# A decoder block in one kernel: the MLP's up product by Strassen's seven block products, with the squared values stored to DRAM and read back for the down product

## The chip, the cores and the metric

The kernel is one program on one core of a Trainium2 chip. It uses TensorE (PE, matmuls into PSUM), VectorE (DVE), ScalarE (ACT), and SyncE (SP) as the queue that issues the DMAs. GpSimd (POOL) only prepares constants. The metric is device time in microseconds, the median of several executions. One more execution was profiled; the rows below come from it.

## What is computed

A hybrid decoder block over 1024 tokens of width 1024: two attention mixers side by side, gates, an output projection with a residual, and an MLP with squared ReLU and a residual. The change touches the second half:

```python
mixed = jax.nn.sigmoid(ga) * ya + jax.nn.sigmoid(gb) * yb
x = x + mixed @ w_out[l]                       # (1024, 1024) @ (1024, 1024)
h = _rms_norm(x, norm_mlp_g[l])                # y * rsqrt(mean(y * y) + 1e-6) * g
x = x + jnp.square(jax.nn.relu(h @ w_up[l])) @ w_down[l]   # 1024 -> 4096 -> 1024
return _rms_norm(x, norm_final_g)
```

All tensors are float32.

## The kernel before

**Data.** Everything is held transposed: 128 features on the partitions, 1024 tokens along the free dimension, so the width of 1024 is eight chunks of 128x1024. `kp` (in `keep`) is the residual in that form, chunk m at `kp[:, m, :]`. A matmul takes a 128x128 weight block and moves 512 tokens (one PSUM bank). PSUM is four tensors `PS[0]` to `PS[3]` of two banks each.

**Precision.** Each operand is split in a high part (a cast to fp32r on ScalarE, `split_hi2`, `mlp_in_hi`) and a low part (value minus high part, on VectorE, `split_lo2`). A product takes three matmuls: high by high, high by low, low by high. So a 1024-deep product of 128 output features for 1024 tokens is 8 x 3 x 2 = 48 matmuls.

**Output projection.** Eight chunks n. Per chunk TensorE transposes a column chunk of x (`x_chunk`, L775), then runs the 48 matmuls (`split_products`, L529). ScalarE copies the transposed x to `kp` (L1143). VectorE adds the product (L1477), ScalarE squares the chunk (L1153), VectorE adds the square to an accumulator (L1485). Chunks 0 to 3 of the MLP's input are split as they come, 4 to 7 after the last chunk (L1136, L1480), since their place is the projection's input until then. Weights come through a ring of four slots (`raw_at`, `wsp_at`).

**MLP.** Eight blocks of 512 hidden features. In a block, four hidden chunks j (L529; the very first by `products_by_chunk`, L518, which takes the input chunks one by one), alternately in `PS[0]` and `PS[1]`. VectorE takes the ReLU and scales by the inverse root mean square (L1496); ScalarE squares (L1164) and casts (L1167); VectorE makes the low part (L1499). Then the down products of these four hidden chunks: for each of eight output chunks m 24 matmuls into `PS[2 + m % 2]` (L837), which VectorE adds to `kp` (L1511). The blocks after the first stand in a loop. The mean square is two 512-column matmuls with a constant matrix (`mean_square`, L798), which leaves the mean on all partitions; then a root on ScalarE (L1156) and a 1024-wide reciprocal on VectorE (L1488).

**The end.** In the last block VectorE also sums the squares of the result (L1516, squares L1178). Eight one-column matmuls give the mean per token (L851), `kp` is transposed back (L857), VectorE scales (L1531), and SyncE stores.

**What sets the order.** It is written out by hand. Each engine runs its own list in order, and the lists meet at semaphores: `w_hi`, `w_lo` (weights split), `w_used` (a chunk's products done), `resid`, `acc_ok`, `u_r`, `u_hi`, `u_lo`, `dn_add`. An instruction that waits holds up all behind it on its engine, and the same holds for SyncE's list of DMAs.

## Time and profile before

| | us |
|---|---|
| median of three runs | 1749.26 (1747.21 to 1750.57) |
| the profiled execution, its own time | 1750.55 |
| its span, first to last instruction | 1748.4 |
| TensorE busy / VectorE busy / ScalarE busy | 1669.4 / 862.9 / 682.0 |
| output projection to the end of the last down product | 931.3 to 1725.9 |
| mean granted TensorE clock | 0.987 |

The span counts from the first to the last instruction, the execution's own time also what lies around it. The granted clock is the share of full speed (2.4 GHz) that TensorE was allowed; 0.50 is 1.2 GHz. Busy time of TensorE is that of pipelined matmuls with modelled ends, so the distance between starts in the chain of waits tells more of its pace than the mean duration of one.

### The profile page before, as it was taken

How to read it: one execution, taken by the hardware profiler on the slowest of the kernel's cores; microseconds unless marked ns; L12 is line 12 of the kernel's file. 1: busy time of each engine (PE TensorE's matmuls, PEld its weight loads, DVE VectorE, ACT ScalarE, POOL GpSimd, SP SyncE). 2: the span in 40 equal slices, each digit the busy share in tenths (PEclk: the TensorE clock that was granted, in tenths of full speed). 3: DMA queues.
4: the chain of work that ended last, by engine and by line, in shares of the span. 5: the costliest groups of instructions: out<-in, count | busy, mean ns of one | idle time of the engine just before them, and what ended most of it. 6: DMA issues, size and time to landing. Idle time of an engine off the chain costs nothing.

```text
span 1748.4 us, 22421 instructions
## 1 busy us (share of the span) xinstructions
PE 1669.4 (95%) x8188; PEld 1372.0 (78%) x8188; DVE 862.9 (49%) x1738; ACT 682.0 (39%) x1484; POOL 4.1 (0%) x20
## 2 busy tenths in 40 slices
PE   6999898897999999999999999999999999999997
PEld 5777677674788887788888888888888888888886
DVE  5788888865666666421226344232323333333345
ACT  6467767773666666411114222121212121212121
POOL 0000000000000000000000000000000000000000
PEclk9999999997899999999999999999999999999999
DMA  5210100110020100112123302111111111111102
GB/s 181 78 33 25 37 25 25 37 37 1 13 61 26 49 13 22 34 43 57 42 76 101 109 26 72 49 48 48 48 48 48 48 48 48 48 48 48 36 12 96
DMA packets 126109, 84.93 MB, mean 49 GB/s; under 512 B 2888, under 2 KB 122696, under 8 KB 125904
## 3 DMA queue, kind: packets, MB, share of 16 engines
q1 hardware_dynamic: 126032, 83.94, 16.0%
q8 instruction: 44, 0.72, 0.2%
q14 instruction: 33, 0.27, 0.0%
HBM read 79.70 MB, written 4.23 MB: 48 GB/s over the span
## 4 chain that ended last, share of the span: by engine, by line
PE 81%; DVE 9%; ACT 5%; issue 4%; DMA 0%; ACTq 0%; DVEq 0%; SPq 0%
PE ps L529 36%; PE ps L837 20%; PE ps L573 12%; PE ps L645 4%; PE ps L612 2%; DVE work L1281 2%; PE ps L623 2%; PE ps L518 1%; ACT work L994 1%; DVE ps L1302 1%; DVE o_nat L1324 1%; ACT tmp L986 1%; DVE tmp L1266 1%; DVE work L1309 1%; ACT tmp L950 1%
## 5 line engine op out<-in xcount | busy, mean ns | idle before, releaser
L573 PE MATMUL ps<-hspl,wsp 128*128 128x512 f32 x1536 | 426.3, 411 | 8.3 <-ACT tmp L950 6.6
L573 PEld LDWEIGHTS ps<-hspl,wsp 128*128 128x128 f32 x1536 | 268.1, 191 | 55.0 <-ACT tmp L950 8.4
L529 PE MATMUL ps<-hspl,wsp 128*128 128x512 f32 x1176 | 276.3, 392 | 0.6 <-ACT keep L1016 0.6
L529 PEld LDWEIGHTS ps<-hspl,wsp 128*128 128x128 f32 x1176 | 222.4, 189 | 47.1 <-issue 0.8
L837 PE MATMUL ps<-hspl,wsp 128*128 128x512 f32 x768 | 177.4, 390 | 0.0
L837 PE MATMUL ps<-hspl,work 128*128 128x512 f32 x768 | 175.4, 389 | 0.0
L1511 DVE TENSOR_TENSOR keep<-keep,ps 128x1024 f32<-128x1024 f32 x64 | 78.2, 1221 | 193.5 <-PE ps L837 192.5
L837 PEld LDWEIGHTS ps<-hspl,wsp 128*128 128x128 f32 x768 | 143.6, 188 | 32.6 <-DVE keep L1511 2.6
L837 PEld LDWEIGHTS ps<-hspl,work 128*128 128x128 f32 x768 | 144.2, 188 | 29.9
L529 PE MATMUL ps<-work,wsp 128*128 128x512 f32 x648 | 153.5, 390 | 0.0
L645 PEld LDWEIGHTS ps<-work 128*128 128x128 f32 x856 | 112.5, 192 | 47.9 <-issue 38.2
L645 PE MATMUL ps<-work 128*128 128x128 f32 x856 | 122.9, 277 | 21.3 <-DVE o_nat L1324 20.3
L529 PEld LDWEIGHTS ps<-work,wsp 128*128 128x128 f32 x648 | 121.7, 188 | 25.7 <-issue 0.5
L1164 ACT ACTIVATE tmp<-tmp 128x1024 f32<-128x1024 f32 x32 | 33.9, 1060 | 264.4 <-DVE tmp L1496 264.4
L529 PE MATMUL ps<-hspl,work 128*128 128x512 f32 x576 | 136.9, 390 | 0.0
L986 ACT ACTIVATE tmp<-ps,negmax 128x128 f32<-128x128 f32 (+7 forms) x160 | 87.5, 547 | 125.8 <-DVE negmax L1302 124.1
L1309 DVE TENSOR_TENSOR work<-ps,work 128x128 fp32r<-128x128 f32 (+3 forms) x192 | 84.5, 454 | 102.6 <-ACT work L994 100.0
L529 PEld LDWEIGHTS ps<-hspl,work 128*128 128x128 f32 x576 | 107.8, 188 | 22.2
L1496 DVE SCALAR_TENSOR_TENSOR tmp<-ps,tmp 128x1024 f32<-128x1024 f32 x32 | 39.2, 1224 | 172.5 <-PE ps L529 172.5
L969 ACT ACTIVATE work<-tmp 64x128 fp32r<-64x128 f32 x320 | 113.2, 354 | 5.9
L1281 DVE SCALAR_TENSOR_TENSOR work<-tmp,work 64x128 fp32r<-64x128 f32 x320 | 101.3, 316 | 9.3 <-ACT work L969 1.8
L529 PE MATMUL ps<-work 128*128 128x512 f32 x384 | 92.2, 389 | 0.0
(158 smaller groups left out, 1737.7 us busy)
## 6 DMA issues: line engine op xcount, KB each, us to landing
raw<-in_w_in SPq DMA_DIRECT2D x47, 512.0 KB, 3.6
raw<-in_w_up SPq DMA_DIRECT2D x16, 512.0 KB, 4.0
tmp<-in_w_up SPq DMA_DIRECT2D x16, 512.0 KB, 4.0
raw<-in_w_down SPq DMA_DIRECT2D x16, 512.0 KB, 3.3
tmp<-in_w_down SPq DMA_DIRECT2D x16, 512.0 KB, 3.3
keep<-in_x SPq DMA_DIRECT2D x8, 512.0 KB, 6.6
fbias<-f_rows SPq DMA_DIRECT2D x8, 512.0 KB, 5.0
tmp<-in_x SPq DMA_DIRECT2D x8, 512.0 KB, 4.4
```

The lines of the kernel that those rows point to most:

```text
L529: ins = pe.matmul(ps[:, cols], w(wp, k), mv(mp, k)[:, cols], start=(k == 0 and n == 0), stop=(k == ks - 1 and n == 2))
L573: ins = pe.matmul(psp(u, g), wsp[:, c % 2, wp, k * P:(k + 1) * P], hspl[:, mp, k, cols], start=(n == 0), stop=(n == 23), skip_group_check= ...
L612: ins = pe.matmul(oo, lt, rh, start=(m == 0), stop=(m == len(ops) - 1), skip_group_check=True)
L623: ins = pe.transpose(PS[2][:, (u % 2) * HALF + (k - a) * P:(u % 2) * HALF + (k - a + 1) * P], probs(G)[:, k * P:(k + 1) * P], ident[:])
L645: ins = pe.matmul(o, pt[:, G % 2, part, n * P:(n + 1) * P], v_nat[:, j, s % 2, :, :].rearrange("p s d -> p (s d)"), start=(part == 0 and n ...
L837: ins = pe.matmul(PS[2 + m % 2][:, cols], wsp_at(m // 2, wp)[:, a:a + P], hid[:, mp, f, cols], start=(f == 0 and n == 0), stop=(f == 3 and ...
L969: act.activation(tile_view(q_st[dst:dst + 64, G % 3, 0, :], t), tile_tokens(q_raw(t)[row:row + 64], t, s // 2), ACT.Copy, scale=-QSCALE).t ...
L986: act.activation(probs(G)[:, 0:n * P], psc[G % 2][:, 0:n * P], ACT.Exp, bias=negmax[:, c:c + 1], scale=-1.0, accum_out=rowsum[:, c:c + 1]) ...
L1281: dve.scalar_tensor_tensor(out=tile_view(q_st[dst:dst + 64, G % 3, 1, :], t), in0=tile_tokens(q_raw(t)[row:row + 64], t, s // 2), scalar=- ...
L1309: dve.tensor_tensor(pt[:, G % 2, 1, a * P:b * P], PS[2][:, (u % 2) * HALF:(u % 2) * HALF + (b - a) * P], pt[:, G % 2, 0, a * P:b * P].bitc ...
L1496: dve.scalar_tensor_tensor(out=tmp[:, 0, :], in0=PS[j % 2][:], scalar=0.0, in1=tmp[:, 3, :], op0=ALU.max, op1=ALU.mult).then_inc(u_r, 1)
L1511: dve.tensor_tensor(kp[:, m, :], kp[:, m, :], PS[2 + m % 2][:], ALU.add).then_inc(dn_add, 1)
```

## The change

**Up product.** The 1024x1024 input H is taken as 2x2 blocks: feature chunks k and k + 4 (k = 0 to 3), left and right 512 tokens. The weights of two neighbouring hidden chunks (q, 16 such pairs) are 2x2 blocks too: a11, a12 for the first chunk and a21, a22 for the second, each 512 x 128. Instead of eight block products (96 matmuls) there are seven of 12 matmuls each, P1 to P7, in Winograd's form with 4 sums of weights (s1 to s4, `sums`), 4 sums of H (`h_t1` to `h_t4`, once), and 7 sums of results. Some sums of results are made by TensorE itself, which adds a product to what the bank holds; the others by `copy_s1`, `copy_s2`, `copy_s3` on ScalarE and `up_c22`, `up_c12` on VectorE. The product order of each q reaches over three pairs (`up_products`). All sums of the weights and of H are made of whole values, then split in a high and a low part (`form_hi`, `form_lo`, `h_hi`, `h_lo`).

**Hidden values.** After the ReLU with the scale (`up_r..`, VectorE) and the square (`square_..`, ScalarE) each 128x512 quarter is stored to the DRAM tensor `hidden`. `kp` serves as room for these, so the residual chunks are stored to `x_mid` in the output stage and read back (`reload`) after the up stage.

**Down stage.** After all of the up stage, eight blocks of four hidden chunks, read from DRAM and split again (`hidden_hi`, `hidden_lo`). The 24 matmuls per output chunk and block stay; they go through all four PSUM tensors in turn, and an add has three further chunks' time.

**Inverse root.** The mean square is eight one-column matmuls with the squares as weights; the root and the reciprocal work on 128x8; eight fp32 matmuls of the broadcast column with the identity (`spread_rstd`) put it on all partitions.

**Output stage.** The chunk order is 0, 4, 1, 5, 2, 6, 3, 7, so pairs k, k + 4 become ready and their sums are made on the way. The weights use two slots. The last chunk runs with k outermost and frees `hspl` piece by piece (`o_used`) for the forms t13 and t4b. The MLP loops are written out instead of looped. The stages before the output projection keep their instructions and order.

Core of the diff:

```diff
+def up_products(n):
+
+    if n == 0:
+        order = [(0, P1), (0, P2), (0, P6), (0, P5)]
+    elif n < UP:
+        order = [(n, P1), (n - 1, P7), (n - 2, P3), (n, P6), (n - 1, P4), (n, P2), (n, P5)]
+    else:
+        order = [(n - 1, P7), (n - 2, P3), (n - 1, P4), (n - 1, P3)]
+    return [x for x in order if x[0] >= 0]
...
+            for n in range(UP):
+                q = n + 2
+                if q < UP:
...
+                if n >= 1:
+                    store_u22(n - 1)
+                if q < UP:
...
+                        sp.wait_ge(a_lo, A_FORM[n, 2])
+                    load_a(q, "a21")
+                    if n == 1:
+                        sp.wait_ge(hf_lo, H_FORM["t4b", 3])
+                    load_a(q, "a22")
+                elif n == UP - 1:
+                    sp.wait_ge(done, PRODUCT[UP - 1, P6])
+                    load_hidden(2)
+                    load_hidden(3)
+                if n >= 2:
+                    store_u12(n - 2)
+                if n >= 1:
+                    store_u21(n - 1)
+                sp.wait_ge(done, PRODUCT[n, P2])
+                if q < UP:
+                    load_a(q, "a12")
...
                 if n == 0:
-                    products_by_chunk(PS[0], ring_w(0), h_at, m_lo, 0).then_inc(w_used, 1)
+                    products_by_chunk(PS[0], w_of(c), h_at, m_lo, 0).then_inc(w_used, 1)
                     x_chunk(0)
-                else:
-                    split_products(PS[n % 2], ring_w(n), h_at, KC).then_inc(w_used, 1)
+                elif n < KC - 1:
+                    split_products(PS[n % 2], w_of(c), h_at, KC).then_inc(w_used, 1)
+                else:
+                    for k in range(KC):
+                        for half in range(2):
+                            cols = slice(half * HALF, (half + 1) * HALF)
+                            for i, (wp, mp) in enumerate(((0, 0), (0, 1), (1, 0))):
+                                ins = pe.matmul(PS[n % 2][:, cols], w_of(c)(wp, k), h_at(mp, k)[:, cols],
+                                                start=(k == 0 and i == 0), stop=(k == KC - 1 and i == 2),
+                                                skip_group_check=True)
+                        if k == KC - 1:
...
                 pe.wait_ge(xres, KC)
+                for i in range(8):
+                    ins = pe.matmul(PS[2][:, i:i + 1], tmp[:, 1, i * P:(i + 1) * P], mean_w[:, 0:1], start=True, stop=True)
+                ins.then_inc(mean_done, 1)
...
+            def spread_rstd():
+
+                pe.wait_ge(rstd_ok, 1)
+                for i in range(8):
+                    ins = pe.matmul(PS[2][:, i * P:(i + 1) * P], xrstd[:, i:i + 1].broadcast_to((P, P)), ident[:],
+                                    start=True, stop=True)
...
+            def product(q, j):
+
+                b = form_place(j)[0]
+                pe.wait_ge(a_lo, A_FORM[q, b])
+                if j == P1:
+                    if q < 2:
+                        pe.wait_ge(resid, KC - 1)
+                    else:
+                        pe.wait_ge(c21_ok, q - 1)
+                elif j == P2 and q < 2:
+                    pe.wait_ge(xres, KC)
+                elif j in (P2, P6):
+                    pe.wait_ge(s1_ok, q + 1)
+                elif j == P5:
+                    if q < 2:
+                        pe.wait_ge(resid, KC)
+                    elif q < 4:
+                        pe.wait_ge(rstd_out, 1)
+                    else:
+                        pe.wait_ge(c12_ok, q - 3)
+                elif j == P7:
+                    pe.wait_ge(s2_ok, q + 1)
+                elif j == P4:
+                    pe.wait_ge(s3_ok, q + 1)
+                else:
+                    pe.wait_ge(c22_ok, q + 1)
...
+                    if q == 0:
+                        pe.wait_ge(hf_lo, H_FORM[{P1: "b11", P2: "b21", P6: "t2", P5: "t13", P7: "t13", P4: "t4b",
+                                                  P3: "t4b"}[j], k])
+                    for m, (wp, mp) in enumerate(((0, 0), (0, 1), (1, 0))):
+                        ins = pe.matmul(o, a_part(q, j, wp)[:, k * P:(k + 1) * P], b_block(j, mp, k),
+                                        start=((j in (P1, P5) or j == P2 and q < 2) and k == 0 and m == 0), stop=(k == 3 and m == 2),
+                                        skip_group_check=True)
+                ins.then_inc(done, 1)
+
+            for n in range(UP + 1):
+                for q, j in up_products(n):
+                    product(q, j)
+                    if (q, j) == (0, P6):
+                        mean_square()
+                    if (q, j) == (1, P1):
...
+
+            for i in range(8 * FF_BLOCKS):
+                b, g = i // 8, i // 2
+                o = PS[DN_BANKS[i % 4]]
...
+                elif i == 3:
+                    pe.wait_ge(c12_ok, UP)
+                else:
+                    pe.wait_ge(dn_add, i - 3)
...
-            with pe.Fori(1, FF_BLOCKS) as b:
-                mlp_block(b, False)
-
+                    for f in range(4):
+                        if i % 8 == 0 and half == 0:
+                            pe.wait_ge(dh_lo, 4 * b + f + 1)
+                        for n, (wp, mp) in enumerate(((0, 0), (0, 1), (1, 0))):
+                            a = f * 256 + (i % 2) * P
+                            ins = pe.matmul(o[:, cols], dn_w[g % 4][:, wp, a:a + P], dn_h[(4 * b + f) % 8][:, mp, cols],
+                                            start=(f == 0 and n == 0), stop=(f == 3 and n == 2))
+                ins.then_inc(dn_done, 1)
 
             pe.wait_ge(facc, KC)
...
+            for n in range(KC):
+                m = OUT_ORDER[n]
+                act.wait_ge(xct_done, n + 1)
+                act.wait_ge(m_lo, KC if n else 1)
+                act.copy(kp[:, m, :], PS[2 + n % 2][:]).then_inc(xres, 1)
+                if n >= 1:
+                    scale(n - 1)
+                if n in (2, 4, 6):
+                    for what in ("b11", "b21", "t2"):
+                        h_hi(what, n // 2 - 1)
+                if n + 2 < KC:
+                    split_hi(CH_OUT + n + 2)
+                if n == 3:
+                    for b in range(3):
+                        form_hi(0, b)
...
+            for k in range(3):
+                h_hi("t13", k)
+            h_hi("t4b", 0)
+            form_hi(1, 0)
+            scale(KC - 1)
+            h_hi("b21", 3)
+            copy_s1(0)
+            h_hi("t2", 3)
+            square_mid(KC - 1)
+            h_hi("t13", 3)
+            copy_s2(0)
+            act.wait_ge(mean_eps, 1)
+            act.activation(xstat[:], xstat[:], ACT.Sqrt).then_inc(mean_root, 1)
+            form_hi(1, 1)
+            for k in range(1, 4):
+                h_hi("t4b", k)
+            act.wait_ge(rstd_done, 1)
+            act.copy(kp[:, 0, :], PS[2][:]).then_inc(rstd_out, 1)
...
+            for n in range(1, UP):
+                copy_s1(n)
+                if n + 1 < UP:
+                    form_hi(n + 1, 0)
+                else:
+                    weights_hi(0)
+                    weights_hi(1)
+                copy_s3(n - 1)
+                square_22(n - 1)
...
+            def sums(q):
+
+                a = {x: a_block(q, x) for x in ("a11", "a12", "a21", "a22", "s1", "s2", "s3", "s4")}
+                dve.wait_ge(a_in[q % 4], 64 * (q // 4 + 1))
+                if q >= 2:
...
+            def residual(n):
+                m = OUT_ORDER[n]
                 dve.wait_ge(w_used, CH_OUT + n + 1)
                 dve.wait_ge(xres, n + 1)
-                dve.tensor_tensor(kp[:, n, :], kp[:, n, :], PS[n % 2][:], ALU.add).then_inc(resid, 1)
...
+            for n in range(KC - 1):
+                if n in (2, 4, 6):
+                    k = n // 2 - 1
+                    h_t2a(k)
+                    h_t2b(k)
+                    h_lo("b11", k)
+                    h_lo("b21", k)
+                    h_t4(k)
+                    h_lo("t2", k)
+                    h_t1(k)
...
+                        form_lo(0, b)
+                residual(n)
+                if n + 2 < KC:
+                    split_lo(CH_OUT + n + 2)
+                add_square(n)
+            h_lo("b11", 3)
+            for k in range(3):
+                h_lo("t13", k)
+            h_lo("t4b", 0)
+            sums(1)
+            form_lo(1, 0)
+            residual(KC - 1)
+            h_t2a(3)
+            h_lo("b21", 3)
+            h_t2b(3)
+            h_t4(3)
+            h_lo("t2", 3)
+            h_t1(3)
+            h_t3(3)
+            add_square(KC - 1)
+            h_lo("t13", 3)
...
+            def up_c12(q):
+                dve.wait_ge(done, PRODUCT[q, P3])
+                dve.wait_ge(s2_ok, q + 1)
+                after(dve, u12_out, 16 * q)
+                add(u12, bank_c(q), s2[q % 2]).then_inc(c12_ok, 1)
...
+            for n in range(1, UP):
+                if n + 1 < UP:
+                    sums(n + 1)
+                up_c22(n - 1)
+                if n + 1 < UP:
+                    form_lo(n + 1, 0)
+                else:
+                    weights_lo(0)
+                    weights_lo(1)
+                up_r22(n - 1)
+                if n >= 2:
+                    up_c12(n - 2)
+                form_lo(n, 2)
+                if n >= 2:
+                    up_r12(n - 2)
+                up_r21(n - 1)
+                if n + 1 < UP:
+                    form_lo(n + 1, 1)
+                else:
+                    hidden_lo(0)
+                    hidden_lo(1)
+                up_r11(n)
+            hidden_lo(2)
...
+            weights_lo(3)
+            for g in range(4 * FF_BLOCKS):
+                pair = DN_PAIRS[g % 4]
+                if g + 4 < 4 * FF_BLOCKS:
+                    hidden_lo(g + 4)
+                if 2 <= g and g + 2 < 4 * FF_BLOCKS:
```

The places where the order of instructions changed most follow. Names: `up_b`, `up_t` are split sums of H; `a_hi`, `a_lo` the split weight forms; `hf_lo`, `a_lo`, `s1_ok`, `done` semaphores.

TensorE before, from the end of the output projection, through the mean square, into the second up chunk:

```order
L529 MATMUL ps<-hspl,work 128x512 x47
L518 MATMUL ps<-work,wsp 128x512 [waits h_lo,w_lo,resid]
L518 MATMUL ps<-work,wsp 128x512 x5
...
L518 MATMUL ps<-hspl,wsp 128x512 [waits h_lo]
L518 MATMUL ps<-hspl,wsp 128x512 x5
L798 MATMUL ps<-tmp,mean_w 128x512 [waits xres,acc_ok]
L798 MATMUL ps<-tmp,mean_w 128x512
L529 MATMUL ps<-work,wsp 128x512 [waits w_lo,resid]
```

TensorE after, the product P2 of q = 0 (its last piece of H), the start of P6, then the start of P1 of q = 1 and the spread:

```order
L1084 MATMUL ps<-up_b_60,a_hi_0_71 128x512 [waits hf_lo]
L1084 MATMUL ps<-up_b_60,a_hi_0_71 128x512
L1084 MATMUL ps<-up_b_60,a_lo_0_77 128x512
L1084 MATMUL ps<-up_b_61,a_hi_1_72 128x512 [waits hf_lo,s1_ok,a_lo]
...
L1084 MATMUL ps<-up_b_59,a_hi_0_74 128x512 [waits resid,a_lo]
...
L1043 MATMUL ps<-ident,xrstd 128x128 [waits rstd_ok]
L1043 MATMUL ps<-ident,xrstd 128x128 x7
```

Where eight pieces of input could be taken as they came, the second product now waits in its last quarter for the piece that the last output chunk completes.

VectorE before, the two last residual adds (L1477) with the four last low parts of the input behind them:

```order
L1469 TENSOR_TENSOR wsp<-raw,wsp 128x1024 [waits w_hi]
L1477 TENSOR_TENSOR keep<-keep,ps 128x1024 [waits xres,w_used]
L1485 TENSOR_TENSOR tmp<-tmp 128x1024 [waits acc_ok,sq_ok]
L1469 TENSOR_TENSOR work<-tmp,work 128x1024 [waits w_hi]
L1477 TENSOR_TENSOR keep<-keep,ps 128x1024 [waits xres,w_used]
L1480 SCALAR_TENSOR_TENSOR hspl<-keep,gm_g,hspl 128x1024 [waits h_hi] x4
```

VectorE after, between the same two adds and just behind the second:

```order
L1856 TENSOR_TENSOR up_t13_0_63<-keep_51,up_t13_0_63 128x1024 [waits hf_hi]
L1856 TENSOR_TENSOR up_t13_1_64<-keep_51,up_t13_1_64 128x1024 [waits hf_hi]
L1856 TENSOR_TENSOR up_t13_2_65<-keep_51,up_t13_2_65 128x1024 [waits hf_hi]
L1856 TENSOR_TENSOR up_t4b_0_67<-keep_51,up_t4b_0_67 128x1024 [waits hf_hi]
L1856 TENSOR_TENSOR a_raw1_1_87<-a_raw1_2_88 128x512 [waits xct_done,a_in1]
L1856 TENSOR_TENSOR a_raw1_2_88<-a_raw1_0_86,a_raw1_2_88 128x512 [waits a_sum]
L1856 TENSOR_TENSOR a_raw1_1_87<-a_raw1_1_87,a_raw1_0_86 128x512
L1856 TENSOR_TENSOR a_raw1_2_88<-a_raw1_0_86,a_raw1_1_87 128x512 [waits w_used,a_sum]
L1886 TENSOR_TENSOR a_lo1_0_80<-a_raw1_0_86,a_hi1_0_74 128x1024 [waits a_sum,a_hi]
L1856 TENSOR_TENSOR keep_51<-keep_51,ps1 128x1024 [waits xres,w_used]
L1856 TENSOR_TENSOR up_t2_62<-tmp_56,keep_51 128x512 [waits h_scaled]
L1856 TENSOR_TENSOR up_b1_60<-tmp_56,up_b1_60 128x512 [waits hf_hi]
```

Four splits of H, the four sums of q = 1 and its first split stand ahead of the last residual add; one weight split stood there before.

## Rows read from the trace of the kernel before

**Rows 1.** The page: busy time, share of the span, instructions of each engine.

```profile
PE 1669.4 (95%) x8188; PEld 1372.0 (78%) x8188; DVE 862.9 (49%) x1738; ACT 682.0 (39%) x1484; POOL 4.1 (0%) x20
```

**Rows 2.** The chain that ended last: start us, us, what.

```profile
1013.98 0.87 PE ps L775 x8
1014.85 10.92 PE ps L529 x48
1025.77 10.88 PE ps L518 x48
1036.65 1.72 PE ps L798 x4
...
1202.19 43.52 PE ps L529 x192
1245.71 43.77 PE ps L837 x192
...
1725.94 0.02 issue
```

**Rows 3.** Waits from 1010 to 1748: engine line, waited for, us, times, longest.

```profile
PEld ps L837 <- DVE keep L1511: 2.6, 7, 0.4
```

**Rows 4.** Stretches: us, busy time (count) per engine, granted clock, DMA share, GB/s.

```profile
1071.00:1700.00 629.00, 628.96 (x2768) 518.66 (x2767) 211.17 (x177) 120.32 (x117) 0.00 (x0) 1.00 0.15 45
```

**Rows 5.** Groups by shape: line, engine, operation | busy us, mean ns | idle before.

```profile
L1469 DVE TENSOR_TENSOR work<-tmp,work 128x1024 fp32r<-128x1024 f32 x36 | 43.7, 1217 | 0.3 <-DVE tmp L1488 0.2
L1202 DVE TENSOR_TENSOR wsp<-raw,wsp 128x512 fp32r<-128x512 f32 x58 | 40.0, 689 | 1.3 <-ACT wsp L876 0.7
L1309 DVE TENSOR_TENSOR work<-ps,work 128x512 fp32r<-128x512 f32 x48 | 32.5, 690 | 48.3 <-ACT work L994 48.3
L950 ACT COPY tmp<-ps 128x512 f32<-128x512 f32 x64 | 37.9, 592 | 38.5 <-PE ps L573 33.1 <-DVE tmp L1266 5.4
L1131 ACT CAST work<-tmp 128x1024 fp32r<-128x1024 f32 x36 | 37.6, 1047 | 137.6 <-PE ps L837 137.6
L1136 ACT ACTIVATE hspl<-keep,gm_g 128x1024 fp32r<-128x1024 f32 x4 | 4.3, 1142 | 7.6 <-PE ps L529 7.6
```

**Rows 6.** DMA issues (KB each, us to landing), and the output's window as in rows 4.

```profile
raw<-in_w_up SPq DMA_DIRECT2D x16, 512.0 KB, 4.0
raw<-in_w_down SPq DMA_DIRECT2D x16, 512.0 KB, 3.3
out_y<-tmp SPq DMA_DIRECT2D x6, 512.0 KB, 2.8
1740.00:1742.00 2.00, 1.90 (x17) 1.59 (x16) 2.00 (x3) 0.00 (x0) 0.00 (x0) 1.00 1.01 406
```

**Rows 7.** TensorE after three gaps (timeline: start, us), and windows around them.

```profile
407.97 5.11 PE L707 MATMUL ps<-ident,work 128*8 128x128 f32 x24 [4.21 <-DVE work L1399]
405.00:408.00 3.00, 0.03 (x1) 0.04 (x2) 1.39 (x7) 1.24 (x3) 0.00 (x0) 0.66 0.00 0
408.00:411.00 3.00, 3.00 (x15) 1.85 (x16) 0.00 (x0) 0.00 (x0) 0.00 (x0) 0.50 0.00 0
411.00:414.00 3.00, 3.00 (x15) 1.77 (x13) 0.89 (x1) 0.89 (x1) 0.00 (x0) 0.71 0.00 0
464.71 1.22 PE L573 MATMUL ps<-hspl,wsp 128*128 128x512 f32 x2 [1.92 <-ACT tmp L950]
462.00:465.00 3.00, 1.08 (x6) 0.80 (x6) 2.21 (x6) 2.93 (x8) 0.00 (x0) 0.83 0.01 3
468.00:471.00 3.00, 3.00 (x14) 2.52 (x12) 1.21 (x5) 0.00 (x0) 0.00 (x0) 0.53 0.00 0
1729.58 2.94 PE L851 MATMUL ps<-mean_w,tmp 128*128 128x1 f32 x16 [3.66 <-DVE tmp L1516]
1730.00:1732.00 2.00, 2.00 (x13) 2.00 (x12) 0.00 (x0) 0.00 (x0) 0.00 (x0) 0.58 0.00 0
1736.00:1738.00 2.00, 2.00 (x15) 2.00 (x14) 1.73 (x2) 0.00 (x0) 0.00 (x0) 0.72 0.64 262
```

741 lines of the change are left out of this document (529 added, 212 removed).

## The prediction

> **What bounds the kernel now.** The page comes first: TensorE is busy for 95% of the span [rows 1]. The chain of waits in order of time says where that matters. From the output projection to the last down product it consists of TensorE alone: chunk after chunk of 48 matmuls, then per MLP block 192 up matmuls and 192 down matmuls, eight times, until 1725.94 us [rows 2]. The last output chunk ends at 1025.77; from there to 1725.94 are 700.2 us, and this is the stretch that the change rewrites. 43.52 / 192 = 0.2267 us is the price of one 128x512 matmul, and the stretch holds 3072 of them: 696.4 us. The rest is 1.72 us for the mean square, and about 2 us of down blocks that take 43.77 instead of 43.52, whose cause is the row of waits: the weight load waits 7 times, 2.6 us in all, for VectorE's add [rows 3]. The windows say that this stretch ran at granted clock 1.00 with VectorE busy a third and ScalarE a fifth of the time [rows 4]. So matmuls taken away are time taken away, as long as the other engines keep up.
>
> **The sum, part by part.** I work against the profiled execution's own time, 1750.55 us (span 1748.4 and 2.15 around it), and go to the median at the end.
>
> Up products. Per pair of hidden chunks (call it q, 16 of them) there are seven products of 12 matmuls, 84 where there were 96. 16 x 12 = 192 fewer, x 0.2267 = **-43.5 us**. The Trainium skill, TensorE: Matmul & The Clock Gate, "Part 1: The HAM clock gate", gives columns / 2.4 GHz plus 2.5 ns as the warm distance; by it 512 columns would be 0.216 us and the saving 41.4. The trace shows 0.2267, so the sum does without that.
>
> Down products. 1536 before and after, but the add has four banks of lag instead of two, and 5.4 us per bank (24 x 0.2267). The 7 waits of rows 3 go, nothing comes: **-2.0 us** (eight blocks x 0.25). What could be late here is hidden values or weights. Per two banks (10.9 us) ScalarE has two 1024-wide casts (2.1 us), VectorE two subtractions and two adds (4.9 us at 1.22) [rows 5], and the loads of the next block are issued a block ahead: 43.5 us for four loads of 3 to 4 us each [rows 6]. Covered. Tail after the last product: same work, 0.
>
> VectorE and ScalarE in the up stage. At 0.69 us for 512 columns, from PSUM or not, and 1.22 for 1024 [rows 5], one q costs VectorE ten 512-wide operations, two of 1024 and one of 1536 (taken as 1.22 + 0.53): 11.1 us. ScalarE: seven of 512 at 0.59, two at 1.05, one of about 1.5: 7.7 us. The products take 19.04. Throughput is no limit, so latency decides. I laid one q out with these prices (0 at the start of the first product, 2.72 apart). Copy of s1: needed at 8.2, done at 3.4. Copy of s3: needed at 10.9, done at 6.1. The bank for the next q's first product: needed at 19.0, free at 14.3. Split weights for q+1: first form at 8.0, second at 16.2, needed at 19.0 and 27.2; the third at 12.6 of its own q, needed at 21.8. The last weight load of q+2 leaves at about 16.5 and needs some 4 us [rows 6], which puts the sums at 1.5 of the next q; it could be 7 us later before the copy of s3 behind it delays a product. No TensorE wait comes out: **0 us**, 0.04 per product at most (112 products, 4.5 us) as the upper end.
>
> The output stage. Eight chunks, 11.8 us each; now VectorE and ScalarE also form the block sums of the activation. Pairs add up to 9.2 us of VectorE per chunk, the chunk with the weight sums of q=0 to 10.6. In sequence VectorE runs up to 7.6 us behind in chunk 4 and is back in step in chunk 6; the residual and split are needed a whole chunk later. **0 us** there.
>
> The junction, where the cover ends. Let 0 be the end of the last output chunk. Ahead of the last residual VectorE now has queued: three t13 splits and one t4b split, which wait for casts that wait for the chunk's own sixth k piece (-2.7); four sums; one weight split. By rows 5 these end at -0.4, 0.8, 3.6 and 4.8. Residual 6.0, scaling on ScalarE (1.14) 7.2, cast 7.8, split 8.6. TensorE does P1 (2.7) and three quarters of P2 (4.8) and then needs this last piece: a wait of **3.8 us**. Before, the same data were ready in time, since the chunks were consumed one by one [rows 2].
> The clock. After a gap of 4.2 us, one of 1.9 us and the 3.7 us in the tail the windows fall to 0.50, the lower of the two levels (1.2 GHz) [rows 7]. From their means (a window of 3 us at 0.83 holds 1.0 us at the low level) each low stretch lasted about 6.8 us; matmuls ran in 4.8, 6.1 and 6.8 us of it, at half speed, so 2.4 to 3.4 us were lost. I take **3.1 us**. The delay hides the next wait: at full clock P6 would end at 12.0 and wait 1.3 us for the squares, ready at 13.3; at the low level it ends at 15.1. Without any drop the two would cost 1.3 in place of 3.1.
> Mean square in eight one-column matmuls: the same operation in the tail took 2.94 us, half of it at the low clock [rows 7]. I take **2.9** (from 1.7, the price of the old form [rows 2], to 3.5); the old form goes, **-1.7**.
> The inverse root by TensorE: eight fp32 matmuls of 128 columns. No row has this. The old mean moved 2 x 512 fp32 columns in 1.72 us [rows 2] and this moves 8 x 128 of them: **1.75** (below 3.5, the same at the low clock). The 1024-wide reciprocal and root leave VectorE and ScalarE, where they were hidden.
> After it: copy 1.05, add and scale 2 x 0.69, square 0.6, copy of s1 0.6 = 3.6 us, and only P7 (2.7) runs meanwhile: **0.9 us**.
> Sum at the junction: 3.8 + 3.1 + 2.9 + 1.75 + 0.9 = 12.5.
>
> Leaving the up stage: the fifth down bank needs the first add, 21.8 us after the last up product. In between lie the last add, scale, square and store of q=15, six reloads of the residual and the next hidden rows, 4 MB in all; output rows of the same shape moved at 406 GB/s [rows 6]. Covered, 0.
>
> Total: -43.5 - 2.0 - 1.7 + 12.5 = -34.7, so 1715.8 for a profiled execution. The median before lies 1.3 under its profiled one: **1714.5 us**. Lower end: no clock drop (-1.8) and the mean at its cheapest (-1.2), so 1711.5, and 2.5 less if VectorE is earlier at the residual than laid out: 1709. Upper end of this case: +4.5 for the handovers: 1719.
>
> **The rivals.**
> Low clock through the whole junction. The one-column matmuls and the waits around them give the array little to do, and the clock might stay at 0.50 until full products run on. For it: three drops after modest gaps in rows 7. Against it: P5 and P1 are 24 full-width matmuls without a gap. The three products and the spread between 18 and 28 would take 9.9 us longer and swallow the wait of 0.9: **1723.5**.
> A recurring wait in every q (the side that is slower). Place: the SyncE queue, in order, stores u22, u12 and u21 before it may load the next a12; the sums wait for it, then the copy of s3, then P4. Price: up to 7 us of lateness nothing; beyond that each us counts 14 times, and from 1.9 us on each gap also drags the clock down (3 us). 14 x (1.9 + 3) = 69: **1784**. It decides against the change from 2.5 us per q. For it: eight transfers and their receipts in one queue. Against it: 2 MB per 19 us is a quarter of what the tail moves [rows 6], and loads landed in 3 to 4 us at twice the size.
> Short groups drag the clock. The seven products change bank every 12 matmuls. If each q had one drop like those of rows 7, 16 x 3.2 = 51: **1766**. In the trace the down stage changes bank half every 12 matmuls too, at clock 1.00 [rows 4], so only waits could do it. The Trainium skill, TensorE: Matmul & The Clock Gate, "A second HAM failure mode: psum-queue depth-cycling", describes just this, a kernel cycling through PSUM banks that idles briefly between groups and swings between clock levels; by that rule the time would be this rival's, and rows 4 speak against it here.
> That the change does not do what it says is excluded for the count: the program's order holds 1344 up matmuls.
>
> **How the numbers follow.** Forecast 0.75, low clock throughout 0.14, recurring wait 0.06, short groups 0.03, 0.02 for something better than the sum. The range for 8 in 10 takes the forecast's own 1709 to 1719 and the first rival with its unknowns: 1708 to 1726. A measurement tells about 0.2% (3.5 us) from no change. Faster: all but the two slower rivals and a part of their milder forms, 0.91; same 0.02; slower 0.07.
>
> **What would show it.** The chain after: 84 matmuls per q in 19.0 us and 43.5 per down block. In the waits: one of TensorE on VectorE of 3 to 5 us about 5 us after the last output chunk, one under 1.5 after the first P7, and no others in 16 q. Windows: the granted clock at 0.5 for one stretch of 4 to 7 us behind the first wait, 1.00 else. The up stage's matmuls must still cost 0.2267. The prediction is wrong if TensorE waits for copies or forms in each q, if the loads on SyncE's queue land later than 11 us, or if the output chunks no longer stand 11.8 apart.

## The result, and the profile after

The changed kernel takes 1711.88 us (1710.07 to 1713.81, four runs) against 1749.63 of the kernel before in the same session: a ratio of 0.9783, 95% interval 0.9771 to 0.9795. Two later comparisons of the same kernel, e0_after and e10_after_again below, gave 1713.76 against 1749.07 and 1713.67 against 1750.3. So the change saves 35.3 to 37.8 us; 34.7 had been worked out. The forecast of 1714.5 us lies 2.6 above the first of the three medians and 0.7 and 0.8 above the others.

Its profiled execution took 1710.07 us (span 1708.3, mean granted clock 0.987). The page first: busy time of each engine, which answers to [rows 1], and two DMA issues of the new stages (KB each, us from issue to landing), which answer to [rows 6].

```profile
PE 1623.1 (95%) x8024; PEld 1337.6 (78%) x8024; DVE 970.9 (57%) x1917; ACT 749.7 (44%) x1602; POOL 4.1 (0%) x20
...
hidden<-keep SPq DMA_DIRECT2D x64, 256.0 KB, 2.3
...
dn_h_raw<-hidden SPq DMA_DIRECT2D x32, 512.0 KB, 6.4
```

TensorE is busy 46 us less, VectorE 108 us more, ScalarE 68 us more, and TensorE's share is still 95%. The bound did not move. The chain in order of time (start us, us, what) shows where, as [rows 2] did:

```profile
927.36 10.89 PE ps L748 x48
...
1026.37 1.23 DVE keep L1856
...
1027.62 1.16 ACT tmp L1403
...
1029.49 0.66 DVE up_b L1856
...
1030.20 6.37 PE ps L1084 x15
1036.57 1.68 PE ps L1036 x16
1038.25 5.59 PE ps L1084 x24
...
1048.75 0.58 ACT keep L1451
...
1049.46 288.60 PE ps L1084 x1272
1338.07 348.17 PE ps L1118 x1536
```

1272 matmuls in 288.60 us are 0.2269 each, and 1536 in 348.17 are 0.2267. Fifteen of the sixteen pairs pass as one piece, without another engine in it. What is not a product lies between 1021.48, where the last output chunk ends, and 1049.46. All waits of TensorE between 920 and 1690 (line, waited for, us, times, longest), as in [rows 3]:

```profile
PE ps L1084 <- DVE up_b L1856: 3.8, 1, 3.8
PE ps L1124 <- DVE f_acc L1856: 3.7, 1, 3.7
PE ps L1084 <- ACT keep L1451: 1.1, 1, 1.1
```

The second is the tail's, which was there before. The windows, as in [rows 4] and [rows 7]: us, busy time (count) of PE, PEld, DVE, ACT, POOL, then granted clock, DMA share, GB/s.

```profile
1054.00:1338.00 284.00, 284.00 (x1255) 235.24 (x1254) 159.64 (x193) 115.72 (x155) 0.00 (x0) 1.00 0.38 122
1338.00:1686.00 348.00, 348.00 (x1537) 288.10 (x1535) 153.20 (x131) 64.81 (x65) 0.00 (x0) 1.00 0.27 96
...
1027.00:1030.00 3.00, 0.00 (x0) 0.00 (x0) 1.78 (x3) 2.25 (x3) 0.00 (x0) 0.85 0.01 3
1030.00:1033.00 3.00, 2.80 (x7) 2.22 (x8) 2.76 (x6) 1.58 (x2) 0.00 (x0) 0.50 0.00 0
1033.00:1036.00 3.00, 3.00 (x9) 2.32 (x8) 3.00 (x3) 1.05 (x1) 0.00 (x0) 0.51 0.01 3
```

From the end of the last output chunk to the last down product: 700.2 us before, 1686.24 - 1021.48 = 664.8 now, so **-35.4** where the sum said -34.7. The profiled executions differ by 40.5; of the other 5.1 us, 4.1 lie ahead of the first output chunk (931.50 before, 927.36 here), in stages that the change does not touch. In the profiles of the experiments this chunk starts anywhere from 929.6 to 932.7. So below, kernels are compared by **S**, the time from the start of the first output chunk (L748 in the chain) to the end of the last down product: 794.4 before, 758.9 after. S leaves out that scatter; three profiles of the same kernel gave 758.9, 757.7 and 757.7. So the 1710.07 us of this execution owe some 4 us to those earlier stages and not to the change.

### The profile page after: what moved, and what is told of

Same layout as the page of the kernel before. It is cut to its first block, busy times and chain, and to the rows that moved or that the text cites. A ratio compares the mean times of both kernels' runs of the same rounds, so it can differ in the third digit from the quotient of the medians.

```text
span 1708.3 us, 22294 instructions
## 1 busy us (share of the span) xinstructions
PE 1623.1 (95%) x8024; PEld 1337.6 (78%) x8024; DVE 970.9 (57%) x1917; ACT 749.7 (44%) x1602; POOL 4.1 (0%) x20
## 4 chain that ended last, share of the span: by engine, by line
PE 79%; DVE 10%; ACT 5%; issue 5%; DMA 0%; ACTq 0%; DVEq 0%; SPq 0%
PE ps L1118 20%; PE ps L1084 18%; PE ps L759 17%; PE ps L803 12%; PE ps L875 4%; PE ps L842 2%; DVE work L1669 2%; PE ps L853 2%; ACT work L1266 1%; DVE ps L1690 1%; DVE o_nat L1712 1%; ACT tmp L1258 1%; DVE tmp L1654 1%; PE ps L748 1%; DVE work L1697 1%
## 5 line engine op out<-in xcount | busy, mean ns | idle before, releaser
L803 PE MATMUL ps<-hspl,wsp 128*128 128x512 f32 x1536 | 423.1, 408 | 8.4 <-ACT tmp L1222 6.8
L1118 PE MATMUL ps<-dn_h,dn_w 128*128 128x512 f32 x1536 | 348.3, 389 | 0.0
L1118 PEld LDWEIGHTS ps<-dn_h,dn_w 128*128 128x128 f32 x1536 | 288.4, 188 | 59.8
L803 PEld LDWEIGHTS ps<-hspl,wsp 128*128 128x128 f32 x1536 | 266.2, 190 | 54.7 <-ACT tmp L1222 8.6
L759 PE MATMUL ps<-hspl,wsp 128*128 128x512 f32 x960 | 222.6, 392 | 0.6 <-ACT keep L1288 0.6
L759 PEld LDWEIGHTS ps<-hspl,wsp 128*128 128x128 f32 x960 | 181.1, 189 | 38.4 <-issue 0.8
L875 PE MATMUL ps<-work 128*128 128x128 f32 x856 | 122.5, 276 | 21.2 <-DVE o_nat L1712 20.1
L1084 PE MATMUL ps<-up_b,a_hi 128*128 128x512 f32 x384 | 120.5, 395 | 4.9 <-DVE up_b L1856 3.8
L842 PE MATMUL ps<-work 128*128 128x256 f32 (+3 forms) x384 | 88.8, 326 | 3.1 <-issue 2.1
L1084 PEld LDWEIGHTS ps<-up_b,a_hi 128*128 128x128 f32 x384 | 73.3, 191 | 21.0 <-DVE up_b L1856 4.2
L853 PE MATMUL ps<-ident,tmp 128*128 128x128 f32 x428 | 73.7, 274 | 10.2 <-issue 6.9
L1084 PE MATMUL ps<-up_t,a_hi 128*128 128x512 f32 x256 | 79.1, 390 | 0.0
L1084 PE MATMUL ps<-up_t4b,a_hi 128*128 128x512 f32 x256 | 78.8, 389 | 0.0
```

What stands on the lines that cost most here:

```text
L759: ins = pe.matmul(ps[:, cols], w(wp, k), mv(mp, k)[:, cols], start=(k == 0 and n == 0), stop=(k == ks - 1 and n == 2))
L803: ins = pe.matmul(psp(u, g), wsp[c % 2][:, wp, k * P:(k + 1) * P], hspl[:, mp, k, cols], start=(n == 0), stop=(n == 23), skip_group_check= ...
L842: ins = pe.matmul(oo, lt, rh, start=(m == 0), stop=(m == len(ops) - 1), skip_group_check=True)
L853: ins = pe.transpose(PS[2][:, (u % 2) * HALF + (k - a) * P:(u % 2) * HALF + (k - a + 1) * P], probs(G)[:, k * P:(k + 1) * P], ident[:])
L875: ins = pe.matmul(o, pt[:, G % 2, part, n * P:(n + 1) * P], v_nat[:, j, s % 2, :, :].rearrange("p s d -> p (s d)"), start=(part == 0 and n ...
L1084: ins = pe.matmul(o, a_part(q, j, wp)[:, k * P:(k + 1) * P], b_block(j, mp, k), start=((j in (P1, P5) or j == P2 and q < 2) and k == 0 and ...
```

## The experiments

Theory: TensorE's products are the bound everywhere, so each of them costs 0.2267 us, and all other loss is at the junction, where VectorE reaches the last residual late. Rivals: a wait in every pair lies close behind, the low clock has nothing to do with the gap, the last residual's own chain and not the queue ahead of it makes the wait, and the form of the inverse root does not matter. Line numbers move by a few where an edit adds lines.

| run | median us | ratio to before (95%) | S |
|---|---|---|---|
| e0_after | 1713.76 | 0.979 (0.9771 to 0.9808) | 757.7 |
| e1_fill | 1715.15 | 0.9802 (0.9785 to 0.9818) | 759.1 |
| e2_sums_late | 1712.22 | 0.9789 (0.9773 to 0.9806) | 754.6 |
| e3_junction | 1707.97 | 0.9762 (0.9746 to 0.9779) | 752.6 |
| e4_eighth | 1754.63 | 1.0024 (1.0014 to 1.0035) | 799.4 |
| e5_load_late | 1717.75 | 0.9814 (0.9795 to 0.9834) | 763.1 |
| e6_load_later | 1754.7 | 1.0033 (1.0022 to 1.0043) | 796.8 |
| e7_old_root | 1721.99 | 0.9838 (0.9822 to 0.9855) | 764.3 |
| e8_two_banks | 1715.0 | 0.9798 (0.978 to 0.9815) | 759.8 |
| e9_junction_2 | 1706.4 | 0.9747 (0.9734 to 0.976) | 751.8 |
| e10_after_again | 1713.67 | 0.979 (0.9777 to 0.9803) | 757.7 |

**The changed kernel again**, as the base for the others.

> The changed kernel once more, as the base that the other runs of this chip are read against. Expected 1712 us, as measured first; executions scatter by some 3.5 us, since the clock drops in the attention stage, which the change leaves alone, fall differently from one execution to the next. If the scatter came from the new stages, their windows would differ between two profiles of this same kernel; the theory expects the stretch from the first up product to the last down product to be 664.8 us again, within 1 us, and the scatter to lie ahead of it.

> The changed kernel unaltered, beside the run before it on the same chip. 1712 to 1714 us; 757 to 759 us from the first output chunk to the last down product. Its low stretch at the junction is either 3.4 or 6.8 us long, as the two profiles so far have it.

The waits are the same 3.8 and 1.1 us. The stretch at the low clock is not: here is a piece of e10_after_again behind the wait, and two windows of it.

```profile
1035.57 5.20 PE ps L1084 x15
```

```profile
1034.00:1037.00 3.00, 1.43 (x3) 1.16 (x4) 2.64 (x4) 2.09 (x5) 0.00 (x0) 0.72 0.01 3
1037.00:1040.00 3.00, 3.00 (x11) 2.37 (x10) 2.95 (x4) 1.66 (x2) 0.00 (x0) 0.71 0.00 0
```

Fifteen matmuls at 0.2267 take 3.40 us. They took 6.37 in the first profile (a low stretch of some 6.8 us by its windows: 0.9 + 3 + 2.94), and 5.20 here (0.28 x 3 x 2 + 0.29 x 3 x 2 = 3.4 us low). Of the other profiles with this 3.8 us wait, e4, e5 and e8 show 6.06 to 6.13, and e0, e6 and e7 show 5.12 to 5.17. The same gap cost 1.7 to 3.0 us of clock, and nothing in the junction's code up to that point differs between the cases. So the expectation for e0_after missed: the stretch from the first up product to the last down product was 663.5 us in e0_after and e10_after_again, not 664.8 within 1, and the 1.2 us between them lie in this low stretch, a part of the change. The larger scatter, 4 us and more, does lie ahead of it.

**An eighth product.** Each pair but the first computes its first product twice (the first copy is overwritten).

```diff
                 o = bank_b(q) if j == P2 else bank_c(q) if j in (P5, P3) else bank_a(q)
+                if j == P1 and q >= 1:
+                    for k in range(4):
+                        for m, (wp, mp) in enumerate(((0, 0), (0, 1), (1, 0))):
+                            pe.matmul(o, a_part(q, j, wp)[:, k * P:(k + 1) * P], b_block(j, mp, k), start=(k == 0 and m == 0),
+                                      stop=(k == 3 and m == 2), skip_group_check=True)
```

> In 15 of the 16 pairs the 12 matmuls of P1 are run twice (the second time they start the bank anew, so the values are the same). That gives the count of matmuls of a plain product, 8 x 12, and leaves every sum, copy, cast, load and store as it is. Theory (TensorE is the bound of the up stage, and each matmul costs 0.2269 us): 180 x 0.2269 = 40.8 us more, 1753, which is the gain of the seven products undone. Rival (the copies, casts and the store queue have become a bound of their own close behind): part of the 40.8 falls into waits that exist already and the time is below 1745; the trace of the changed kernel shows none such after the first pair.

180 matmuls more at 0.2267 are 40.8 us; S grew by 40.5 to 41.7, the median by 40.9 to 42.8, and the kernel is no faster than the one before. The low stretch behind the first wait was the long one here too: with its fifteen matmuls taken off both (6.06 here, 6.37 in the first profile) the two S differ by 40.8. No wait appears in the pairs. So the gain of the up stage is the eighth product that is left out.

**Weights later.** The last weight load of a pair (a12) waits for the next first product (5.4 us later), or for the product two behind (10.9 us later). Diff of the second; in the first the wait is always for PRODUCT[n, P1].

```diff
+                if 1 <= n < UP - 1:
+                    sp.wait_ge(done, PRODUCT[n, P1] if n == 1 else PRODUCT[n - 2, P3])
+                    load_a(n + 1, "a12")
                 if n >= 1:
...
                 if q < UP:
-                    load_a(q, "a12")
+                    pass
```

> The last weight load of each pair (a12 of q + 2) is issued 5.4 us later, behind P1 of the next pair in place of P2. Theory (it could land some 9 us later before anything reaches TensorE: it lands 2.9 us after its issue, the cast and the copy of s3 behind it are not needed until 10.9 us into the pair): no wait of TensorE in the up stage, 1712, 288.6 us for the stretch of 1272 matmuls. Rival (a recurring wait is near): a wait in each of 14 pairs and at least 14 us more.

> The same load 10.8 us later, behind P3 (the third product of the next pair). Theory: it lands at 11.1 us into the pair, the cast and the copy of s3 end at 12.75, P4 wants it at 10.9, so TensorE waits 1.9 us at P4 in each of 14 pairs, and up to 1 us more where VectorE, now behind, frees the bank for the next P1: 26 to 40 us. If each such gap also lowers the clock (2 to 3 us each) it is 55 to 80 us. So 1738 to 1752 without the clock and 1767 to 1792 with it. Rival (a later load is caught up with by the other engines): under 10 us.

At 5.4 us, S grew by 4.2 to 5.4, against the forecast of nothing. The chain says that it is one event and not a recurring one, and two rows of SyncE from the timeline say why:

```profile
1051.45 3.00 PE ps L1087 x12
1054.45 2.54 issue
1057.00 3.19 PE ps L1087 x9
```

```profile
1050.90 0.34 SPq L584 DMA_DIRECT2D hidden<-keep  x1
1051.29 1.04 SPq L551 DMA_DIRECT2D a_raw<-in_w_up  x2
```

The wait stands in the first pair alone. Its load does not leave when the first product of q = 1 ends (1045.7) but at 1051.3, since the edit puts it behind the first pair's store of u11 on SyncE's list, and that store leaves only at 1050.90, after the spread, the first scaling and the square. The load lands at 1055.37, and P4 starts at 1057.00. The clock drops behind the wait (0.54 in the window 1058 to 1060), which is the rest. In the other pairs nothing waits. In one of them the load leaves at 1145.94 and lands at 1150.00, the copy of s3 ends at 1151.53, and the product that needs its bank starts at 1153.90: 2.4 us to spare.

At 10.9 us it recurs. A row of the waits, and ScalarE and TensorE in one pair:

```profile
PE ps L1087 <- ACT keep L1470: 24.3, 14, 1.9
```

```profile
1101.39 1.05 ACT L1446 CAST a_hi<-a_raw 128x1024 fp32r<-128x1024 f32 x1 [7.35 <-DMA a_raw<-in_w_up]
1102.34 0.58 ACT L1470 COPY keep<-ps 128x512 f32<-128x512 f32 x1
...
1103.07 0.70 PE L1087 MATMUL ps<-up_t4b,a_hi 128*128 128x512 f32 x2 [1.73 <-ACT keep L1470]
```

This is the rival's path: load, then a cast on ScalarE that stands in the queue ahead of the copy of s3 (L1470 here, L1467 in the changed kernel), then P4. The rival had the sums of VectorE in this path; the cast waits for the load itself (1101.39) and not for them. It lies in the pair at 1103.07 and again at 1124.52, 21.45 us apart where 19.04 are the products. So a pair costs 2.4 us, a little more than its wait of 1.7, since the bank for the next P1 also comes some 0.3 us late (VectorE's L2023). Thirteen such pairs make 31 of the 38 to 39 by which S grew. The rest is the first pair, a shorter wait of 1.2 us in the last one, and one low stretch. By S that is within the 26 to 40 of the expectation; the median, 1754.7, lies 2.7 above its 1752. The surprise is the clock: in 5 us windows from 1060 to 1385 it is 1.00, but for the first pair and one place of two windows, of which this is the first:

```profile
1295.00:1300.00 5.00, 3.13 (x11) 2.50 (x11) 4.73 (x7) 1.53 (x2) 0.00 (x0) 0.79 0.00 0
```

Thirteen gaps of 1.7 to 1.9 us and one of 1.2 brought one drop. A gap of 1.92 us had brought one in [rows 7].

**The old root.** The mean square as two 512-column matmuls (four records in the trace), root and reciprocal 1024 wide, no spread.

```diff
-                for i in range(8):
-                    ins = pe.matmul(PS[2][:, i:i + 1], tmp[:, 1, i * P:(i + 1) * P], mean_w[:, 0:1], start=True, stop=True)
+                for half in range(2):
+                    cols = slice(half * HALF, (half + 1) * HALF)
+                    ins = pe.matmul(PS[2][:, cols], mean_w[:], tmp[:, 1, cols], start=True, stop=True)
...
-                    if (q, j) == (1, P1):
-                        spread_rstd()
```

> The third part of the change undone: the mean square by two 512-column matmuls, the root on ScalarE over 128x1024, the reciprocal on VectorE over 128x1024, no spread by TensorE. Theory (this part pays by what queues behind the 6.55 us reciprocal on VectorE, not on TensorE): TensorE saves 1.65 us, but the reciprocal and the t4b forms behind it end at about 31 us after the last output chunk, the copy of s1 of q = 1 waits for the first result behind them, and the wait ahead of P6 of q = 1 grows from 1.1 to 8 us, with 2 to 3 us of low clock: 5.5 to 9 more, 1719. Rival (the reciprocal is hidden as it was before): 1.6 us less, 1710.

Of its waits the one that grew, and a piece of its chain (start us, us, what):

```profile
PE ps L1085 <- ACT keep L1450: 7.6, 1, 7.6
```

```profile
1044.98 6.47 DVE keep L1978
...
1051.49 3.29 DVE up_t4b L1853 x3
```

S grew by 5.4 to 6.6, the median by 8.2 over e0_after. The chain of waits (second piece) shows why: VectorE's 1024-wide reciprocal takes 6.47 us. Behind it stand three t4b splits and the first add of the pair, and behind these the square and the copy of s1 for which TensorE waits. The wait of 1.1 us became 7.6, and a second low stretch followed (0.50 from 1056 to 1060). So the change's root is part of its gain: without it some 6 us of the 36 are gone. TensorE's own share does not decide this: eight one-column matmuls took 1.68 us where the old form takes 1.73 (1039.86 in the chain), and the spread adds 1.7.

**Two banks of lag in the down stage**, as before the change.

```diff
                 else:
-                    pe.wait_ge(dn_add, i - 3)
+                    pe.wait_ge(dn_add, i - 1)
```

> The down stage waits for the add two banks back in place of four, as before the change. Theory A (the prediction's: the longer lag removed the 0.37 us waits of the kernel before): about one short wait of 0.2 to 0.4 us per block returns, 2 us in all, 350 us for the 1536 down matmuls. Theory B (those waits came from the order within the first pair of banks, where the last hidden chunk's part of bank 0 ended only 2.7 us before the third bank started): no wait returns, 348.2 us, since an add is done 3.9 us after its bank at the latest, and 5.4 are there.

Among the waits of TensorE one is new:

```profile
PE ps L1118 <- DVE keep L1856: 0.8, 1, 0.8
```

The 1536 down products take 1691.35 - 1342.07 = 349.3 us instead of 348.2, all of it at the entry (1364.65), where the first adds still wait for the first hidden rows. The recurring wait of [rows 3] does not come back. So the lag was not what removed it. The trace of the kernel before shows a cause (no run changes the order of that kernel, so this is a reading of its trace), VectorE's first adds in a down block that began at 1245.71 and the weight load that waits for them:

```profile
1255.27 2.58 DVE L1511 TENSOR_TENSOR keep<-keep,ps 128x1024 f32<-128x1024 f32 x2 [3.64 <-PE ps L837]
1256.55 5.54 PEld L837 LDWEIGHTS ps<-hspl,wsp 128*128 128x128 f32 x25 [0.38 <-DVE keep L1511]
```

A block began with its first two groups over hidden chunks 0 to 2 and only then took chunk 3 for both, since chunk 3 came last. The first group was so complete after 18 + 18 + 6 = 42 matmuls (9.5 us), and its bank was wanted after 48 (10.9 us): 1.36 us, and not the 2.7 of the expectation, for an add of 1.22 with its signals. It happened once per block, seven times in the window. In the separate down stage each group of 24 is closed before the next begins, which leaves 5.4 us even with two banks. Theory B is borne out in this; its 348.2 us missed the entry.

**Filling the gap.** Sixteen matmuls without use in the place where TensorE waits.

```diff
                 for k in range(4):
+                    if q == 0 and j == P2 and k == 3:
+                        for _ in range(16):
+                            pe.matmul(bank_b(1), a_part(0, P1, 0)[:, 0:P], b_block(P1, 0, 0), start=True, stop=True)
```

> Sixteen dummy matmuls (128x512, 3.6 us at full clock, into a free bank) stand where TensorE waits 3.8 us for the last piece of b21. They add no result. Theory (the wait costs its own length plus the clock that it drags down): the wait shrinks to 0.2 us, the last piece comes as late as ever (8.7 us behind the last output chunk), and the clock stays at 1.00, so the following matmuls run at full speed: 2.3 to 2.6 us less, 1709.5. The wait for the squares behind P6, hidden now, comes back and takes about 1 of it if the squares are late. Rival (the low clock does not come from this wait): 1712 us, unchanged, with the low window still there.

Its waits of TensorE from 1000 to 1690 beside the 1.1, and a window at the end of the mean square and behind it:

```profile
PE ps L1036 <- DVE tmp L1859: 1.0, 1, 1.0
PE ps L1087 <- DVE up_b L1859: 0.2, 1, 0.2
```

```profile
1040.00:1043.00 3.00, 3.00 (x11) 2.42 (x11) 1.34 (x3) 2.35 (x4) 0.00 (x0) 0.55 0.83 241
```

The expectation failed: S did not shrink. The drop behind the first gap is gone, so it does come from that gap, and the rival is refuted in this. But at full clock the squares are late by 1.0 us, and then the clock fell anyway, behind this small gap and the one-column matmuls (0.55 in the window). One drop was traded for another.

**Weight sums behind the last residual.**

```diff
             h_lo("t4b", 0)
-            sums(1)
-            form_lo(1, 0)
             residual(KC - 1)
...
             h_lo("t13", 3)
+            sums(1)
+            form_lo(1, 0)
             dve.wait_ge(mean_done, 1)
```

> VectorE alone is reordered: the four weight sums of q = 1 and its first low part (4.0 us) stand behind the low part of t13 of chunk 3 and no longer ahead of the last residual add. Theory (the queue ahead of that add makes the 3.8 us wait): the wait at the end of P2 falls to about 0.1 us, the clock does not drop (2.3 us), about 1.3 us of wait for the squares, 0.9 for the first form of q = 1 and 0.2 for the inverse root come instead. In all -3 to -4.5 us: 1708. Rival (the add is late for ScalarE's sake, or the piece's own chain of scale, cast and low part sets the time): 1712, with the wait still over 3 us.

Its waits of TensorE from 1000 to 1690:

```profile
PE ps L1084 <- ACT keep L1451: 1.1, 1, 1.1
PE ps L1036 <- DVE tmp L1856: 0.9, 1, 0.9
PE ps L1084 <- DVE a_lo L1886: 0.4, 1, 0.4
PE ps L1084 <- DVE up_b L1856: 0.3, 1, 0.3
```

Of the 3.8 us 0.3 are left, and 1.3 came in their place (squares 0.9, the split of q=1 0.4). The clock stayed at 1.00. S fell by 3.1 to 4.3 us. It is the sums and the weight split ahead of the residual that made the wait. The median moved by only 1.5 against e0_after, to 1712.22 and not to the expected 1708. That is the number that the rival had given, but the rival's sign, a wait still over 3 us, did not come. The profile of e2 has S = 754.6, inside the forecast of 3 to 4.5 less; why the median moved by less was not followed up, and the scatter of the stages in front (some 3 us) is as large as the difference.

**The junction in another order.** e3 also moves splits of H behind what TensorE needs first, and the copy of s1 of q=1 ahead of the spread's copy; e9 then takes the four sums of q=1 apart and puts them one by one into VectorE's free places.

```diff
+            h_lo("t13", 0)
             h_lo("b11", 3)
-            for k in range(3):
-                h_lo("t13", k)
-            h_lo("t4b", 0)
-            sums(1)
-            form_lo(1, 0)
+            h_lo("t13", 1)
...
+            add(a1["s1"], a1["a21"], a1["a22"]).then_inc(a_sum, 1)
+            h_lo("t13", 2)
             residual(KC - 1)
+            dve.wait_ge(a_sum, 5)
+            add(a1["s3"], a1["a11"], a1["a21"], ALU.subtract).then_inc(a_sum, 1)
...
+            add(a1["s2"], a1["s1"], a1["a11"], ALU.subtract).then_inc(a_sum, 1)
             h_lo("t13", 3)
...
+            add(a1["s4"], a1["a12"], a1["s2"], ALU.subtract).then_inc(a_sum, 1)
+            form_lo(1, 0)
```

> The whole junction in another order, on VectorE and ScalarE: the sums of q = 1 and t13 of chunks 0 and 1 while the last output chunk runs, the last residual add right behind that chunk, then only what P2 and P6 need, the squares ahead of t1 and t3, t4b of chunk 0 behind t13 of chunk 3, and the copy of s1 of q = 1 ahead of the copy of the inverse root. Theory: no wait of TensorE over 0.5 us between the last output chunk and the tail, clock at 1.00 throughout, 3.8 + 2.3 + 1.1 = 7.2 us less: 1704.7. Rival (the junction is bounded by the length of the chain residual, scale, cast, low part, 4.5 us, which P1 and three quarters of P2, 4.8 us, just cover): 1 to 3 us of waits remain, 1707 to 1709.

> The reordered junction, with the four sums of q = 1 spread out: the first where VectorE waits for a cast, the second in the wait for the scaling, the third and fourth with the low part behind the two sums of chunk 3; on ScalarE the cast of the first form behind that of t13 of chunk 2. So the weight load that lands 9.5 us into the last output chunk holds up one short sum and no longer the residual add. Theory: the wait of 1.5 us at the end of P2 goes, one of up to 0.5 us ahead of P1 of q = 1 may come: from the first output chunk to the last down product 751.5 us in place of 752.6, 1707 in all. Rival (the chain residual, scale, cast, low part is just too long): the wait stays above 1 us.

In e3 one wait of 1.5 us was left, and the time, 1707.97, fell in the rival's range. But its cause is not the rival's. The chain shows a load behind it: the sums wait for weights that land at 1023.69, 7.9 us into the last output chunk (e9's expectation says 9.5), and the residual, wanted when that chunk ends at 1026.6, waits behind the sums. The wait, and the chain:

```profile
PE ps L1084 <- DVE up_b L1859: 1.5, 1, 1.5
```

```profile
1019.24 4.45 DMA a_raw<-in_w_up
...
1023.71 0.70 DVE a_raw L1859
...
1029.33 1.14 DVE keep L1859
```

With the sums taken apart (e9) the residual begins at 1024.78, as soon as the last chunk ends, the waits are these (the first is the tail's), and the clock is 1.00 in every window from 1024 to 1054:

```profile
PE ps L1124 <- DVE f_acc L1859: 3.7, 1, 3.7
PE ps L1084 <- issue: 0.3, 1, 0.3
PE ps L1084 <- DVE a_lo L1889: 0.2, 1, 0.2
```

S is 751.8 where 751.5 was expected, 5.9 to 7.1 below the changed kernel's, and the time is 1706.4 us (1704.28 to 1708.59, five runs), 7.3 under e10_after_again, which was timed with it. This is the fastest version: 0.9747 of the kernel before. Of its S, 94.1 are the output chunks and 652.9 the 2880 matmuls at 0.2267. Of the 4.8 left, 3.5 are the mean and the spread, so at most about 1.3 us is still to be had at the junction (an estimate).

## Why the prediction was right, point by point

**Up products, -43.5.** Right. 0.2269 each in 1272 of them, and e4 gives 40.5 to 41.7 for 180 that were put back. The 0.216 us by which the saving would have been 41.4 appeared nowhere.

**Down products, -2.0.** Right in size, wrong in cause, so the size was luck. The step said that four banks of lag in place of two would remove the waits of [rows 3]. With two banks they do not return (e8). By the reading above they came from the order in which a block closed its first two groups, and went because the separate down stage closes each group before the next. The lag is worth 1.1 us, once, at the entry, and this too depends on when the hidden rows come back: in e8 the third add began 21.2 us after the first down product, in the first profile 20.0, where even two banks would have had no wait (an estimate: 20.0 + 1.2 is less than the 21.8 at which the fifth group starts). The reading error: the row names the add that was late, and I took the distance between banks for its cause without looking at when the group in that bank was closed.

**VectorE and ScalarE in the up stage, 0.** Right: no wait in pairs 2 to 16, and none of the 4.5 us for handovers. The slack was given as 7 us of lateness. By e5 it is 5.4 + 2.4 = 7.8, and by e6 10.9 - 1.9 = 9.0 (its load landed in 2.7 us, e5's in 4.1). It holds from the second pair on. In the first, work on SyncE's list that waits for the spread can hold a load up by more than 5 us (e5), which the layout of a steady pair could not show.

**The output stage, 0.** Right. From the start of the first output chunk to the end of the last were 1025.77 - 931.50 = 94.3 us, and are 1021.48 - 927.36 = 94.1 now.

**The junction, 12.5.** It measured 3.80 + 2.97 + 1.68 + 1.70 + 1.08 = 11.2, as follows.
- First wait 3.8: exact. The residual was laid out at +4.8 and began at +4.9 (1026.37). e2 confirms that the sums in front of it are the cause.
- Clock 3.1: 3.0 in this profile, 1.7 to 3.0 over eight. The size is not a property of the gap alone; that the first profile met 3.1 so closely is luck.
- Mean square 2.9: this term was mis-sized. It took 1.68 us. The row taken for it was half at the low clock; the low stretch here ended just ahead of it. The lower bound, 1.7, was the right value at full clock.
- Spread 1.75: 1.70 (1043.68 to 1045.38 in the rows below), from a row of another form by its columns.
- Last gap 0.9: 1.08.
- The hidden wait for the squares, 1.3 at full clock: e2 and e1 show 0.9 and 1.0.

TensorE's timeline at the spread (start us, us, instruction):

```profile
1043.68 1.95 PE L1043 MATMUL ps<-ident,xrstd 128*128 128x128 f32 x16
1045.38 0.71 PE L1084 MATMUL ps<-up_t,a_hi 128*128 128x512 f32 x2
```

So the prediction had 1.3 too much at the junction, nearly all of it in the mean. With the measured 11.2 in its place the sum would be -36.0, and -35.4 was measured. The other 0.6 us stand in no term: the junction's 27.98 us less its 72 products (16.3) are 11.7, so 0.4 lie in the restarts around the gaps (24 matmuls took 5.59 us and not 5.44), and 0.2 in the 1272 matmuls at 0.2269. The two errors go against each other, so the agreement within 0.7 is a little better than the working behind it. With the short low stretch of e0_after the same stretch is 663.5 us, which is -36.6.

**Leaving the up stage, 0.** Right, but closer than "covered" says. The first hidden rows came back at 1352.4, 14.3 us after the first down product, and the first add ran at 1354.63; the fifth group wanted it at 1359.8 (ScalarE's cast and VectorE's adds below). The loads of hidden rows took 6.4 us (median of 32). Four us of cover were left. In the profiles of the experiments the rows came back 14.9 to 17.0 us after the first down product, the latest in e5, where the first add began at 19.2 and 1.3 us were left. With two banks (e8) the cover was gone.

```profile
1352.40 1.05 ACT L1491 CAST dn_h<-dn_h_raw 128x1024 fp32r<-128x1024 f32 x1 [11.47 <-DMA dn_h_raw<-hidden]
...
1354.63 2.35 DVE L1856 TENSOR_TENSOR keep<-keep,ps 128x1024 f32<-128x1024 f32 x2
```

**The rivals.** *Low clock through the junction* (14%): it did not come. Even in e1, where the clock fell near the end of the one-column matmuls (1040.3), it was back at 1.00 by 1043.7, within the next 24 matmuls. *A recurring wait*: its mechanism is real and was made to appear in e6, by a path without the sums; it just starts 8 to 9 us away from where the kernel stands. Its price was over-stated. It counted 3 us of clock for each gap from 1.9 us on, while one drop came in 13 gaps of 1.7 to 1.9. *Short groups*: clock 1.00 over all the pairs, with a change of bank every 12 matmuls. The Trainium skill, TensorE: Matmul & The Clock Gate, "A second HAM failure mode: psum-queue depth-cycling", tells of a kernel that idled between groups as it cycled through banks. This kernel cycles through banks too, but TensorE has no idle time between its groups (284.00 of 284.00 us busy in the window 1054 to 1338). So the condition of that section is not met here, and its swings did not come.

## What to carry to other kernels

Where one engine's matmuls fill the span without a gap, a count of them times the measured distance is a close forecast: 2808 x 0.2267 is 636.6 us, and 636.8 were measured here. The work goes into the places where the sequence starts or ends. Lay out the queue of each helper engine there, instruction by instruction, and move ahead of the late operand only what it needs: here that reordering is worth 6 to 7 us beyond the change. And for a wait on a bank, ask when the group in that bank was closed, before counting how many banks lie between.

## What the runs showed of the chip

- A gap does not set the clock's course by its length alone. A wait of 3.8 us was followed by a low stretch of either about 3.4 or about 6.8 us, four times each in eight profiles, one of 2.5 us (e5) by one of 3.4, 13 of 1.7 to 1.9 us (e6) by one in all, one of 1.5 us (e3) by none, and one of 1.0 us with one-column matmuls behind it by one (e1) in one kernel, while one of 0.9 us was followed by none (e2) in another. What decides between them stays open: no run here separates the length of a gap from its position in time.
- Work moved in front of a stall can move the clock's drop rather than remove it (e1).
- Eight fp32 matmuls of one column took 1.68 us at full clock, nearly as long as two of 512 columns (1.73).
- Loads of 512 KB of hidden rows, which the kernel itself had stored to DRAM, landed in 6.4 us; loads of weights of the same size landed in 3.5. No run shows what makes the difference.
